# Order of the steps inside a round of the attention pipeline: newest unit first

## The reference

```python
for l in range(DEPTH):                       # 2 layers
    xn = rmsnorm(x, norm_mix[l])
    (qa, ka, va, qb, kb, vb, qc, kc, vc, qi, ki, wi, gates) = jnp.split(xn @ w_in[l], offsets, axis=-1)
    o_a = chunk_band_attention(...)          # 8 heads of 64, with a bias table
    o_b = diff_attention(...)                # 4 heads, two softmaxes subtracted
    o_c = dsa_attention(...)                 # 8 heads, 64 keys picked per query by an index score
    g = jax.nn.sigmoid(gates).reshape(b, s, 3, D_MODEL)
    y = g[:, :, 0] * (o_a @ w_up_a[l]) + g[:, :, 1] * (o_b @ w_up_b[l]) + g[:, :, 2] * (o_c @ w_up_c[l])
    x = x + y @ w_out[l]
    x = x + memory_cross_attention(...)      # 4 heads
    x = x + swiglu(...)
```

## Time and profile before

| | |
|---|---|
| median of three runs | 3427.57 us |
| the profiled execution | 3439.49 us |
| its span, first to last instruction | 3437.7 us |
| PE busy | 3149.3 us, 92% |
| VectorE (DVE), ScalarE (ACT), GpSimd (POOL) busy | 48%, 36%, 6% |
| granted TensorE clock, mean | 0.954 of full speed |
| share of PE in the chain that ended last | 82% |

### The profile page before, as it was taken

How to read it: one execution, slowest core, us unless ns; L and a number is a source line. 1 busy time by engine, 2 the same in 40 slices (tenths; PEclk the granted TensorE clock), 3 DMA queues, 4 the chain that set the end, 5 groups by cost and what they waited for, 6 DMA issues and landing times.

```text
span 3437.7 us, 45740 instructions
## 1 busy us (share of the span) xinstructions
PE 3149.3 (92%) x18558; PEld 2638.7 (77%) x18558; DVE 1662.3 (48%) x2638; ACT 1237.3 (36%) x2091; POOL 203.8 (6%) x293
## 2 busy tenths in 40 slices
PE   6897989988798998999997889999999998997899
PEld 6676969977696996777765567777777777784899
DVE  4565555555555655423473555423443335334555
ACT  3344444434444543212243313212232223233443
POOL 1120000012000000000010110000000001001000
PEclk8999999999998999999998899999999998999899
DMA  4533556553354663332331123333333333341454
GB/s 156 164 104 114 176 172 195 203 165 99 102 190 135 221 223 111 110 123 94 115 132 53 35 70 117 114 119 100 108 134 100 110 129 129 105 148 54 135 187 139
DMA packets 264694, 446.02 MB, mean 130 GB/s; under 512 B 16723, under 2 KB 87780, under 8 KB 263716
## 3 DMA queue, kind: packets, MB, share of 16 engines
q1 hardware_dynamic: 260272, 430.80, 38.2%
q10 hardware_dynamic: 4212, 12.29, 1.0%
HBM read 441.98 MB, written 1.05 MB: 129 GB/s over the span
## 4 chain that ended last, share of the span: by engine, by line
PE 82%; DVE 10%; ACT 4%; issue 2%; DMA 2%; POOL 0%; ACTq 0%; DVEq 0%; SPq 0%; POOLq 0%
PE ps L1054 22%; PE ps L1056 21%; PE ps L1055 21%; DVE split L1726 2%; PE ps L1249 2%; PE ps L1085 2%; PE ps L1087 2%; PE ps L1086 2%; PE ps L1197 2%; DVE A L1723 1%; DVE AR L1726 1%; ACT split L1443 1%; PE ps L1208 1%; PE ps L1183 1%; ACT A L1528 1%
## 5 line engine op out<-in xcount | busy, mean ns | idle before, releaser
L1054 PE MATMUL ps<-AR,split 128*128 128x256 f32 (+1 forms) x4784 | 1599.6, 334 | 72.9 <-DVE split L1726 39.3
L1055 PE MATMUL ps<-AR,split 128*128 128x256 f32 (+1 forms) x4784 | 1561.0, 326 | 0.0
L1056 PE MATMUL ps<-AR,split 128*128 128x256 f32 (+1 forms) x4784 | 1560.5, 326 | 0.0
L1726 DVE TENSOR_TENSOR split<-raw,split 128x1024 fp32r<-128x1024 f32 (+1 forms) x728 | 813.0, 1158 | 916.5 <-ACT split L1443 911.1
L1054 PEld LDWEIGHTS ps<-AR,split 128*128 128x128 f32 x4784 | 915.9, 191 | 234.2 <-issue 65.0
L1443 ACT ACTIVATE split<-raw 128x1024 fp32r<-128x1024 f32 (+1 forms) x728 | 682.3, 987 | 854.6 <-PE ps L1056 718.1
L1056 PEld LDWEIGHTS ps<-AR,split 128*128 128x128 f32 x4784 | 917.8, 192 | 82.8
L1055 PEld LDWEIGHTS ps<-AR,split 128*128 128x128 f32 x4784 | 917.6, 192 | 82.0 <-issue 2.6
L1723 DVE SCALAR_TENSOR_TENSOR A<-A,ps 128x256 f32<-128x256 f32 (+1 forms) x196 | 96.9, 508 | 141.2 <-ACT A L1486 132.3
L1726 DVE TENSOR_TENSOR AR<-A,AR 128x256 fp32r<-128x256 f32 (+2 forms) x268 | 144.9, 543 | 25.0 <-ACT AR L1502 7.7
L2194 POOL TENSOR_TENSOR A<-A 128x256 f32<-128x256 f32 (+1 forms) x45 | 40.7, 905 | 1797.4 <-ACT A L1451 1638.2
(11 more groups left out here) (227 smaller groups left out, 2306.2 us busy)
## 6 DMA issues: line engine op xcount, KB each, us to landing
mod<-w_mod SPq DMA_DIRECT2D x288, 256.0 KB, 3.9
raw<-w_in SPq DMA_DIRECT2D x120, 512.0 KB, 4.9
raw<-w_gu SPq DMA_DIRECT2D x80, 512.0 KB, 4.7
raw<-ffn_a_in SPq DMA_DIRECT2D x80, 512.0 KB, 4.6
raw<-ffn_b_in SPq DMA_DIRECT2D x80, 512.0 KB, 4.6
raw<-ret_in SPq DMA_DIRECT2D x48, 512.0 KB, 4.8
raw<-w_down SPq DMA_DIRECT2D x44, 512.0 KB, 5.4
raw<-ffn_a_out SPq DMA_DIRECT2D x44, 512.0 KB, 4.7
```

Of the source, the lines that this page charges most:

```text
L1054: e.matmul(out, wh[:, c, m_], x.hi(k0 + c, a, b), start=first, stop=False)
L1055: e.matmul(out, wh[:, c, m_], x.lo(k0 + c, a, b), start=False, stop=False)
L1056: mm = e.matmul(out, wl[:, c, m_], x.hi(k0 + c, a, b), start=False, stop=last)
L1726: return self.e.tensor_tensor(out, v, hi.bitcast(F32), ALU.subtract)
```

## The change

`newest_first` has two effects in the new code, and its default stays False. Where it is False, the live units now step from the newest (last in `live`) to the oldest, and the list of those still alive is built by inserting at the front, so that it keeps its order. Where it is True (retention) nothing changes. The place of a new unit's scores (the end of the round), the filler's shares, `side` and all buffers stay.

```diff
             parts, still = max(1, len(live)), []
-            for k in range(parts):
+            for k in range(parts) if newest_first else range(parts - 1, -1, -1):
                 if k < len(live) and next(live[k], StopIteration) is not StopIteration:
-                    still.append(live[k])
+                    still.insert(len(still) if newest_first else 0, live[k])
                 owed += per / parts
```

## The result

The changed kernel takes 3379.29 us (median of four runs, 3363.43 to 3388.71) against 3429.88 us of the kernel before on the same chip (3427.07 to 3432.26). The medians differ by 50.6 us. The ratio on record is 0.9842, with a 95% interval from 0.9821 to 0.9863, which is about 54 us less, 47 to 61 by the interval. Forecast were 71.7. Two more comparisons of the same kernel gave 0.9812 (0.9781 to 0.9844) and 0.9840 (0.9820 to 0.9861). All ratios are of fast runs alone; one run in this document was slow, an execution of the kernel with exp last that took 12675 us, and that kernel's median of 3430.37 us would be 3429.77 without it. The profiled execution took 3379.46 us with a span of 3377.7, which is 60.0 us under the span before.

The account below looks back on a forecast made before the run. PE bounds the kernel (busy 92% of the span, 82% of the chain); only its idle and slow time can be won. 54.4 + 2 + 0 + 15.3 = 71.7 us off the median 3427.57 gives 3356 us, range 3333 to 3378.

Parts of the forecast that it names:

- waits of scores, a: Branch a, both layers: PE's scores waiting for exponentials, 27.9 us, would lose 18.7; 3 us left per layer besides second units' waits.
- waits of scores, c: Branch c, both layers: PE's scores waiting for exponentials, 18.4 us, would lose 13.8; 2.3 us left per layer.
- waits of scores, neighbourhood: Neighbourhood attention: of 32.3 us of scores waiting for exponentials, 1.4 + 2.0 + 7.0 would stay and 21.9 go.
- new waits at turns: Neighbourhood attention, rounds with splits: PE's turns would newly wait for ScalarE's copy that frees their bank, about 2 us in all.
- cross attention: Both cross attentions: a turn before the values covers copies, net about 1 us per layer, 2 in all (bounds 0 and 4.6).
- branch b: Branch b: no gain or loss, 0; if the cover of its second exponentials is gone, 31 us lost.
- clock: Half-clock windows in or right behind the waits cost 30.5 us; half of that, 15.3, would be regained (bounds 0 and 30.5).
- What stays: Branch a, neighbourhood and cross attention: second units' scores keep waiting, with one live unit nothing to reorder; 10.6 us in all.
- the same, with gates in place of picks: Branch c's estimate, taken over from branch a's walk through the queues: 13.8 us of 18.4 go.
- signs of being wrong: Waits at L1183 above 50 us, L1197 or L1054 newly waiting over 20 us, or branch b growing by over 3 us.
- The slower rival: Branches a, c, neighbourhood: copies stand behind waiting exponentials, 48 turns wait 2 us each, 96 us; 24 us slower, 3452; chance 0.08.
- Half of it: VectorE's queue stays the bound, waits of 3 to 5 us become 2, clock stays low; 37 to 45 saved, 3387; chance 0.22.

Follow-up runs that it names:

- the kernel with exp last: Against the kernel before, scale, turn, values and low run from newest to oldest unit while exp stays last of the live units' steps; 3430.37 us, ratio 0.9995.

## Why the prediction was right in sign and 18 us too high

The mechanism was right: the waits named were removed, for the most part by the step named; exp alone brings about three quarters of the stages' gain. The 54 us lie near the lower end of the forecast's own range of 50 to 95, and the median of 3379.29 is 1 us above its 3378. By terms, against the profiled executions (59.6 us in the stages, forecast 71.7):

| term | forecast | measured |
|---|---|---|
| waits of scores, a | 27.9 to 9.2 | 27.9 to 6.4 |
| waits of scores, c | 18.4 to 4.6 | 18.4 to 3.4 |
| waits of scores, neighbourhood | 32.3 to 10.4, of it 2 at turns | 32.3 to 7.4 |
| new waits at turns | 2, in that | 4.0 in a, 7.3 in c, 5.3 |
| idle time gained, a, c, neighbourhood | 54.4 | 17.2 + 7.8 + 19.6 = 44.6 |
| cross attention | 2 | 4.0 |
| branch b | 0 | 1.0 |
| clock (measured: what is left) | 15.3 | 10.0 |

- *What stays* was right: the second unit's scores in the neighbourhood attention still wait 1.41 us, those of branch a of the second layer 1.56. In the first layer this profile has no such wait, because the stage's first 2.1 us ran at half clock and PE came to these scores later; the two other profiles of the changed kernel have it, with 1.58, which is the 1.6 us by which their L1183 lies above 23.1. So 1.6 of branch a's gain in the table is chance.
- *Waits of scores* fell further than I said, by 61.4 us in these three stages. The third unit's scores in the neighbourhood attention wait 1.33 and the fourth's 0.56, where I had 1.3 and 0.7.
- *The failed step is branch c:* "the same, with gates in place of picks" gave 13.8 and it was 7.8. I had followed scores, exponentials and copies through the queues and left scale out. It stands behind exp and a share of filler now, and a pair of remainders in that share waits for ScalarE's splits, which wait behind the exponentials. The trace shows it, and with no filler between exp and scale the waits for diagonals were 0, 0 and 0.5 us in three kernels.
- *New waits for copies* were named, by mechanism and place (0.73 and 1.22 us in the neighbourhood attention, forecast 0.5 to 0.7 per pair of splits), but I had none in branch a, where one wait of 2.02 us in each layer stands in the drain. Of the 5.3 us of new waits in the neighbourhood attention 2.0 are for a step of the convolution's filter (L2010).
- *Cross attention* gained twice my estimate.
- *Clock* was mis-sized: 10.0 for 15.3. In the neighbourhood attention 31.7 us at half clock became 7.5; in branch c, where other waits stay, 34.2 became 30.8. The price was wrong rather than the share that clears: PE's busy time at half clock fell from 80.4 to 50.1 us in the stages, and half of the difference is 15.1. But half-clock work does not take quite twice as long here. Matmuls of the filler with 512 columns follow one another by 0.43 us at half clock (from 1838.20 in the trace of the kernel before) and by 0.23 at full clock (from 1840.96); that explains a part, the rest is open.
- *Signs named:* the neighbourhood attention shrank by 25.6 us (near 30 forecast), branch a by 11.3 and 9.2 (some 13), and the mean clock rose from 0.954 to 0.958. None of the signs of being wrong came.
- The rest, from 59.6 to the 54 of the ratio, can't be told from chance: executions of one program differ by more than that ahead of the first attention. For the same reason 7 us were too small for what a measurement can tell; three comparisons of the changed kernel gave ratios that are 0.003 apart, 10 us.

The slower rival did not come about: turns wait 6.0 us for copies in all, not 96. What it says is seen only where splits meet a copy. Half of it was nearest in size among the rivals, but its reason is refuted: scores' waits fell by 73%, not by half.

## What to carry to other kernels

When one written order serves all engines, try first in a round the step on which the scarce buffer of the next round hangs: here whatever stood before it in the queues was added to its chain. Then follow every other step of the round past its new neighbours, the cheap ones too: a step of 0.65 us behind a split that itself waits costs a stall. Where background work is placed matters too: of the three placements tried with exp first and scale second, the one with none between these two and a double share at the round's end was the fastest.

## What was not expected of the hardware

With the same order of instructions and 2.3 us between their idle times, the 113 to 122 us ahead of the first attention ran at a mean granted clock of 0.84 in one execution and 0.92 in another: 38.9 us of them at half clock in the one, 17.1 in the other. That makes most of the 9.6 us between them, 0.3% of the kernel, and hides gains of that size from single runs. In the twelve profiles of this document the stretch, the same code in all, lasts from 112.1 to 122.6 us. The Trainium skill (TensorE: Matmul & The Clock Gate, "What's actually happening") calls the number of matmuls at the low clock run-variable; these two profiles agree, with 134 and 51 matmuls begun at half clock.
